# Products of constants on TensorE ahead of the last up stages of two expert mixtures and of the transposes between them

## What is computed

```
# block 1, its mixture: each token goes to two experts of one group
y = sum over chosen experts e:  weight_e * (silu(h @ w1[e]) * (h @ w3[e])) @ w2[e]
x = layer_norm(ALPHA * x + (1 + g2) * y) * ln2_g + ln2_b
# block 2, its begin and its mixture: each expert takes its 32 best tokens
h = rms_norm(x, norm_mix_g);  p = h @ w_in_2
...
hid = silu(xe @ w_gate[e]) * (xe @ w_up[e]);  ye = (hid @ w_down[e]) * gates
x = x + scatter(ye);  out = rms_norm(x, final_norm_g)
```

## Time and profile before

| | us |
|---|---|
| median of 3 runs | 1619.3 (1618.76 to 1621.59) |
| the profiled execution: its span, first to last instruction | 1619.4 |
| TensorE busy with products | 1319.3 (81%) |
| VectorE, ScalarE, GpSimd busy | 457.8, 284.4, 132.9 |
| mean granted TensorE clock | 0.910 |
| HBM traffic | 316 GB/s over the span |

### The profile page before, as it was taken

One profiled execution on the slowest core, in us unless ns is written; L12 is line 12 of the kernel. 1 busy time (PEld: TensorE's weight loads), 2 busy tenths in 40 slices (PEclk: granted clock), 3 DMA queues, 4 the chain that ended last, 5 costly groups with the idle time before them and its releaser, 6 DMA issues.

```text
span 1619.4 us, 27191 instructions
## 1 busy us (share of the span) xinstructions
PE 1319.3 (81%) x11722; PEld 747.4 (46%) x11722; DVE 457.8 (28%) x968; ACT 284.4 (18%) x634; POOL 132.9 (8%) x289
## 2 busy tenths in 40 slices
PE   5999999999999887778777789888786666765665
PEld 4755887888564332223223278677432222221211
DVE  1246237431463222222222243653510000000001
ACT  0101214650021110111101113342211101100001
POOL 4000013000000000000000004122000000000000
PEclk9999999999999989889988889999998887777878
DMA  9799664122479999999999691310899999999996
GB/s 347 282 388 340 182 242 169 65 104 84 163 317 428 426 429 428 428 428 429 429 429 427 281 339 43 97 55 4 359 414 427 428 428 427 429 429 428 429 426 289
DMA packets 86486, 513.98 MB, mean 317 GB/s; under 512 B 8521, under 2 KB 13050, under 8 KB 61826
## 3 DMA queue, kind: packets, MB, share of 16 engines
q1 hardware_dynamic: 82306, 502.84, 76.5%
q0 software_dynamic: 3424, 9.27, 1.6%
q10 hardware_dynamic: 672, 0.65, 0.1%
HBM read 507.84 MB, written 3.15 MB: 316 GB/s over the span
## 4 chain that ended last, share of the span: by engine, by line
PE 51%; DMA 42%; DVE 3%; issue 2%; ACT 1%; SPq 1%; POOL 0%; DVEq 0%; ACTq 0%
PE ps L1502 41%; DMA ring<-in_exp_w 19%; DMA arena<-in_w_e_down 19%; PE ps L2302 4%; DMA ring<-in_w_e_up 2%; PE ps L1594 2%; DMA ring<-in_w_in 1%; PE ps L2074 1%; PE ps L1750 0%; SPq L650 0%; PE ps L1746 0%; DVE stats L2711 0%; PE ps L1549 0%; PE ps L2315 0%; PE ps L2103 0%
## 5 line engine op out<-in xcount | busy, mean ns | idle before, releaser
L1502 PE MATMUL ps<-ring,arena 128*32 128x512 f32 (+4 forms) x1844 | 266.2, 648 | 101.9 <-DMA ring<-in_exp_w 86.0
L1502 PE MATMUL ps<-ring,hTs 128*32 128x512 f32 (+2 forms) x992 | 214.1, 636 | 39.3 <-DMA ring<-in_w_e_up 24.0
L1502 PE MATMUL ps<-hTs,ring 128*128 128x256 f32 (+2 forms) x1008 | 218.2, 386 | 0.0
L1502 PEld LDWEIGHTS ps<-ring,arena 128*32 128x32 f32 (+1 forms) x1844 | 81.9, 127 | 266.7 <-issue 201.0
L1502 PEld LDWEIGHTS ps<-hTs,ring 128*128 128x128 f32 (+2 forms) x1008 | 184.2, 188 | 30.2 <-issue 5.0
L1502 PE MATMUL ps<-arena,vv 128*32 128x512 f32 (+2 forms) x560 | 92.2, 710 | 91.2 <-DMA arena<-in_w_e_down 84.6
L1502 PEld LDWEIGHTS ps<-ring,hTs 128*32 128x32 f32 (+1 forms) x992 | 75.8, 136 | 149.2 <-issue 105.5
L3127 DVE COPY hTs<-ps 64x512 f32<-64x512 f32 x32 | 22.2, 693 | 259.9 <-PE ps L1502 259.9
L1502 PEld LDWEIGHTS ps<-arena,vv 128*32 128x32 f32 (+2 forms) x560 | 28.2, 143 | 138.7 <-DMA arena<-in_w_e_down 92.1
L1502 PE MATMUL ps<-arena,hTs 128*32 128x512 f32 x480 | 92.0, 618 | 0.0
L1220 ACT COPY arena<-ps 128x512 f32<-128x512 f32 x32 | 18.8, 586 | 388.4 <-PE ps L2052 388.4
(11 more groups left out here) (471 smaller groups left out, 1469.5 us busy)
## 6 DMA issues: line engine op xcount, KB each, us to landing
ring<-in_exp_w SPq DMA_DIRECT2D x92, 2048.0 KB, 22.2
arena<-in_w_e_down SPq DMA_DIRECT2D x28, 2048.0 KB, 25.8
ring<-in_w_e_gate SPq DMA_DIRECT2D x24, 2048.0 KB, 30.7
ring<-in_w_e_up SPq DMA_DIRECT2D x24, 2048.0 KB, 36.3
ring<-in_w_in SPq DMA_DIRECT2D x22, 2048.0 KB, 13.7
ring<-in_ada_w SPq DMA_DIRECT2D x12, 2048.0 KB, 15.5
arena<-in_w_e_up SPq DMA_DIRECT2D x8, 2048.0 KB, 34.3
arena<-in_w_e_gate SPq DMA_DIRECT2D x8, 2048.0 KB, 33.8
```

The costliest lines, as they stand in the source:

```text
L1502: return nc.tensor.matmul(o, lhsT, rhs, start=start, stop=stop)
```

## The change

A helper `spare` is added on TensorE. It issues `count` products of 512 columns into PSUM bank `b`, where nobody reads them. It is called in three places: four products ahead of the last expert's up products in the first mixture (bank 3, identity and constants), seven ahead of the second block's transposes (bank 2, identity and constants), and six ahead of the second half of the last up products of the second mixture (bank 3, identity and the activations `xf`). No other line changes.

```diff
@@ -1501,6 +1501,12 @@
             def mm(o, lhsT, rhs, start=True, stop=True):
                 return nc.tensor.matmul(o, lhsT, rhs, start=start, stop=stop)
 
+            def spare(b, lhsT, rhs, count):
+
+                for _ in range(count):
+                    nc.tensor.matmul(ps[:, b * 512:b * 512 + rhs.shape[1]], lhsT, rhs, start=True, stop=True,
+                                     skip_group_check=True)
+
             def chunk_pair(name, i, wt, c0, src):
                 products(job(name, i), wt, c0, src)
 
@@ -2078,6 +2084,8 @@
             def expert(turn, at, pos, last=False):
 
                 pe.wait_ge(S("xe1_ready"), turn + (at + 1))
+                if last:
+                    spare(3, C("ident"), cst[:, 0:512], 4)
                 up_compact(turn, at, pos)
                 turn_compact(turn, at - 1)
                 if not last:
@@ -2168,6 +2176,7 @@
             wpos[0] = R2
 
 
+            spare(2, C("ident"), cst[:, 0:512], 7)
             half_transposes("h3T", xn2, "mix_normed", 4)
             for i in range(3):
                 n = tile("in2")
@@ -2668,6 +2677,7 @@
             up2(0, e + 1, (0,))
             down2(0, e, (1,))
             combine2(0, e)
+            spare(3, C("ident"), xf[:, 0, 0:512], 6)
             up2(0, e + 1, (1,))
             turn2(0, e + 1)
             down2(0, e + 1)
```

## The result

The changed kernel takes 1623.62 us (median of 20 runs, 1620.42 to 1626.5) against 1619.8 us for the kernel before (20 runs beside it): a ratio of 1.0025, with an interval of 1.0019 to 1.0031. It is slower by about 4 us, where 3.5 us less than before was forecast. Of the three gains that the prediction counts the trace shows two, and something else takes more than they give.

What follows compares the result with a forecast made beforehand. The prediction saw TensorE's chain, at half clock after idle waits, as the bound at the three places, with tile landings limiting the gains. 1.8 + 1.2 + 0.5 = 3.5 us, so 1619.4 - 3.5 = 1615.9 us, range 1613.6 to 1618.4.

Steps and rivals of the forecast that it cites:

- the last term: All later TensorE instructions move, which may change its waits for its own issue: -1 to +1 us, taken as 0.
- Place one: Four spares ahead of the first mixture's last up stage keep the clock full: 1.8 us gained.
- The cut by expert 30's down tile: First mixture: down products wait for this tile, landing at 915.25 us, cutting the up stage's 2.78 us gain to 1.8.
- rival D: Tiles land 1 to 2 us earlier against the chain, so 6.0 us are won, 1613.4 us; chance 0.08.
- Rival A: Waits behind eat more and a median run has less to win: 2.4 us in all, 1617.0 us; chance 0.26.
- Place two: Seven spares ahead of the second block's transposes keep the clock full through the first products: 1.2 us gained.
- 1.0 us left: Second block's transposes: seven spares take 6.5 us of 7.53 us idle, so they are hidden with this room.
- Place three: Six spares ahead of the second mixture's last up half: up stage 1.75 us shorter, 0.5 us gained after a tile wait.
- the down products [...] take 3.64 us: End of the second mixture: the last down products keep this length for both halves of the tile.
- One to one: What the first two places win moves the second mixture's stream earlier and reaches the end in full.
- Rival B: Spares run but the clock falls all the same or rises no sooner: 1619.4 us; chance 0.07.
- C: Slower: spares outlast the waits, at half clock 1.85 us each; about +8 us, 1627 us; chance 0.07.

Runs made afterwards that it cites:

- u44: Kernel before plus 11 products (44 instructions) in the never-taken branch for uneven routing, no spares executed; 1628.81 us, ratio 1.0052.
- p256: Kernel before plus all 17 spares and 53 never-run products, so the mixer's code lies 256 instructions further on; 1616.63 us, ratio 0.9978.
- p1n: Kernel before plus only the four spares of the first place and 240 never-run instructions, mixer's code 256 further on; 1617.68 us, ratio 0.9984.
- u40: Kernel before plus 10 products (40 instructions) in the never-taken branch, no spares executed; ratio 1.0014.
- p2n: Kernel before plus only the seven spares of the second place and 228 never-run instructions, mixer's code 256 further on; 1620.12 us, ratio 0.9993.

## Why the prediction was wrong

**The step that failed** is the last term: "One unknown is left: the added instructions move all later ones in TensorE's program [...] bounds -1 to +1 us, taken as 0." Measured, it is +6.3 us of waits in the changed kernel, +6.5 in u44, and +0.52% of the time in u44, about 8 us with nothing else changed. The bounds had no row behind them. The row that the prediction had the earlier trace rows said that the mixer loses 9.9 us in 10 pieces to its own issue; a bound from it would have been that these waits can all fall away or come twice, -10 to +10 us, and then the sign of the forecast would have been open. The trace of before also had the pattern to see: the waits 256 instructions apart, and a loop whose first run ends 104 records behind one of them. What the runs showed in the term's place is a wait for the program's own code: which products stand 256 instructions apart depends on the position, and at a shift of 44 TensorE needs a block whose transfer comes late (5.0 of the 16.2 us). Why it comes late stays open.

**Place one** held. Taken as 1.8 us; alone it won 2.6 us (0.3 to 4.9 by the interval), of which 1.3 us may be the shorter waits in its mixer. From the start of the up stage to the down products of expert 30 it is 8.10 us before, and 5.28, 5.86 and 5.27 in the changed kernel, p256 and p1n. The cut by expert 30's down tile, on which the 1.8 rests, does occur: in p256 the products wait 1.27 us for it instead of 0.68 for ScalarE. In p1n and in the changed kernel it does not, and the whole gain of the up stage stays, as rival D has it. Rival A is right in one point: the 6.47 us of the earlier trace rows is large. The same stage took 4.96, 5.16, 5.34, 5.92, 5.98, 6.16, 6.18 and 6.37 us in the eight other kernels of this study that have no spares there, so the usual gain is 1.3 to 2.7 us.

**Place two** held, with another balance. Taken as 1.2 us between 0 and 1.5; the traces show 0.8 to 2.3. The clock stayed at 1.00 across both gaps and the transposes (934.60 to 937.90 us, above). By the Trainium skill ("TensorE: Matmul & The Clock Gate", Part 4: PE-mode transpose) the full clock does not engage in transposes; the transposes behind the spares, passed at 1.00, do not bear that out. The prediction's reading of the earlier trace rows was weaker than it says, because other products ran ahead of those transposes too, from 229.60 us on. The "1.0 us left" behind the seven spares was not there: they start 1.57, 1.47 and 1.51 us late by TensorE's own issue, a wait that 7.53 us of idleness covered before; a transfer of code starts 2.4 to 2.5 us ahead of them (last section). They end as the rows are ready, at most 0.2 us behind them (926.93 + 7.53 = 934.46 us, against the transposes at 934.62 in the changed kernel).

**Place three** won nothing. The up stage ended 1.75 us sooner as forecast, relative to its tile. The step "the down products [...] take 3.64 us" failed, and so did the wait for the last down tile as the only loss. TensorE's timeline in the changed kernel, then two stretches of it:

```profile
1595.69 5.42 PE L1507 MATMUL ps<-arena,cst 128*128 128x512 f32 x12
1601.60 3.64 PE L1502 MATMUL ps<-ring,hTs 128*32 128x512 f32 x32 [0.49 <-DMA ring<-in_w_e_up]
...
1608.40 5.48 PE L1502 MATMUL ps<-arena,vv 128*32 128x512 f32 x32 [0.68 <-ACT vv L1453]
```

```profile
1602.00:1605.60 3.60, 3.24 (x32) 0.94 (x24) 0.00 (x0) 0.31 (x1) 0.00 (x0) 1.00 1.00 423
...
1609.40:1612.60 3.20, 3.14 (x20) 0.47 (x16) 0.00 (x0) 0.00 (x0) 0.00 (x0) 0.50 0.04 15
```

The same in p256, its down products and a stretch of them:

```profile
1598.50 5.20 PE L1502 MATMUL ps<-arena,vv 128*32 128x512 f32 x32 [0.68 <-ACT vv L1453]
```

```profile
1599.40:1602.40 3.00, 3.00 (x24) 0.73 (x20) 0.00 (x0) 0.00 (x0) 0.00 (x0) 0.62 0.05 22
```

In all three kernels with these spares the clock falls under the last down products, after the same gaps of 1.43 and 0.68 us that the kernel before has, and there it stayed full. What the up stage wins, the down products give back: 5.2 to 5.5 us instead of 3.64. In p256 they show no wait for a tile at all, so there it is the clock alone. The chain of the changed kernel does go through the last down tile (its landing at 1611.23 us, 2.66 us of products behind it), so there the forecast limit and the clock meet. Why the clock falls there and not before is open; it also fell in two of the kernels without spares (u40 and p2n: 5.06 and 4.98 us), those with the slowest last up stage (6.43 and 6.29 us).

**One to one** held within a spread: from the stream's start to the end it is 480.7 us in before, 479.4 in p256 and 481.4 in the changed kernel (479.4 to 483.2 in all twelve traces), so what the mixer loses reaches the end. **Rival B** is refuted (the clock is full under the up stages and across the transposes), **C** too: no spare ran at half clock, and the spares outlast the waits by at most 0.2 us. C named the right sign for the wrong mechanism. The frame was also loose: executions of this study took 1.8 to 2.9 us more than their spans, so a span of 1619.4 us is a time of about 1621; the signs do not hang on that.

## What to carry to other kernels

Code that is added ahead of a stage of very short instructions moves that stage in the program; where its trace shows waits for issue, count the instructions between them, and bound the cost of moving by those waits both ways. To test a small addition fairly, fill up a branch that is never taken until the later code lies where it lay (here 256 instructions on), and measure the filling alone as well (that of 256 was not run alone here). Spare products do hold the clock through a wait, but ask what the next gap does with it: here they won at two places of three.

## What the runs showed that was not expected

- 44 instructions that are never executed cost 0.52% of the time (u44), and 48 and 68 cost as much; 40, 172 and 196 cost 0.13 to 0.19%. The page of the changed kernel has the transfers of the program itself, 1.08 MB in 66 packets, so 16 KB each:

```profile
q8 instruction: 66, 1.08, 0.3%
```

- The Trainium skill ("Runtime: NRT & Kernel Launch", Instruction fetch mechanics) has code fetched in blocks of 16 KiB, 256 instructions, and calls the crossing mostly hidden. The distance of the waits agrees with it in every trace here. "Mostly hidden" does not, for products this short: a crossing in the mixer costs from nothing to 2.4 us, and up to 5.0 near a loop's end. That the waits are these fetches rests on the distance, the shifts, and the 68 transfers that stand beside them.
- The loop's later runs show waits of 0.3 us only: what was once crossed is not paid again in it. In u44 no transfer of code starts from 1056.3 to 1068.9 us, while the loop runs on.
- The seven spares behind the branch that is not taken start 1.5 us late in all three kernels that have them. A transfer of code stands there too, 2.4 to 2.5 us before the first spare in each of them. That the jump over the branch's code calls for it is likely and was not tried. By the Trainium skill ("Runtime: NRT & Kernel Launch", Instruction fetch mechanics) a taken branch out of the fetched stretch waits for its target, which would agree. The changed kernel from 925.9 to 926.1 us:

```profile
q8 instruction: 1, 0.02, 32.8%
```

- p256, the change with its shift filled up, beats both kernels: 0.9978 (0.9965 to 0.9992) of the kernel before.
